# A hybrid encoder step on one core: products over 640 frames cut as 512 and 128 columns in place of 320 and 320

## The reference

```python
def swiglu(x, wg, wu, wd):
    return (jax.nn.silu(x @ wg) * (x @ wu)) @ wd

def half_ffn_block(x, wg, wu, wd, g, b):
    return layer_norm(ALPHA * x + 0.5 * swiglu(x, wg, wu, wd), g, b)
```

## Time and profile before

| | |
|---|---|
| time, median of 3 runs (lowest to highest) | 2917.87 us (2915.64 to 2918.74) |
| span of the profiled execution | 2920.5 us |
| busy share of the span: PE, PEld, DVE, ACT, POOL | 95%, 90%, 35%, 29%, 31% |
| matmul records, weight load records | 18,936 and 18,936 |
| mean granted TensorE clock | 0.968 of full speed |
| HBM traffic | 82 GB/s over the span |

### The profile page before, as it was taken

How to read it: one execution, slowest core, us unless ns; L and a number is a source line. 1 busy time by engine, 2 the same in 40 slices (tenths; PEclk the granted TensorE clock), 3 DMA queues, 4 the chain that set the end, 5 groups by cost and what they waited for, 6 DMA issues and landing times.

```text
span 2920.5 us, 49217 instructions
## 1 busy us (share of the span) xinstructions
PE 2781.7 (95%) x18936; PEld 2635.1 (90%) x18936; DVE 1026.9 (35%) x1731; ACT 846.2 (29%) x1351; POOL 914.9 (31%) x506
## 2 busy tenths in 40 slices
PE   5999999999888999999999999999999899999998
PEld 4999999898665899999999999997887688999998
DVE  2220225212555722112452212253865554211235
ACT  2221222322653332122232212223246524221222
POOL 2333333332000333333333333333133233333331
PEclk8999999999999999999999999998999999999998
DMA  9222222132347122222212222222130611222221
GB/s 154 72 83 69 72 80 73 57 111 73 131 156 265 58 65 82 76 66 78 79 51 76 81 66 79 83 62 49 44 95 1 147 51 58 74 82 67 77 83 56
DMA packets 396204, 239.64 MB, mean 82 GB/s; under 512 B 14433, under 2 KB 371025, under 8 KB 396113
## 3 DMA queue, kind: packets, MB, share of 16 engines
q1 hardware_dynamic: 396112, 238.48, 29.0%
HBM read 223.46 MB, written 14.98 MB: 82 GB/s over the span
## 4 chain that ended last, share of the span: by engine, by line
PE 88%; issue 3%; DMA 3%; ACT 2%; DVE 2%; POOL 2%; SPq 0%; DVEq 0%; ACTq 0%; POOLq 0%
PE ps L1218 73%; PE ps L1228 3%; PE ps L1311 3%; PE ps L1328 2%; PE ps L1319 1%; DMA raw<-in_ffn_w_gate 1%; PE ps L1361 1%; POOL wl L527 1%; PE ps L1286 1%; PE ps L1391 1%; PE ps L1375 1%; DVE big L888 1%; PE ps L1412 0%; ACT wh L650 0%; PE ps L1418 0%
## 5 line engine op out<-in xcount | busy, mean ns | idle before, releaser
L527 POOL TENSOR_TENSOR wl<-raw,wh 128x1024 fp32r<-128x1024 f32 (+1 forms) x296 | 779.6, 2634 | 1570.8 <-ACT wh L650 1570.8
L1218 PE MATMUL ps<-xh,wh 128*128 128x320 f32 x3488 | 797.6, 310 | 31.0 <-POOL wl L527 30.5
L1218 PE MATMUL ps<-xl,wh 128*128 128x320 f32 x3488 | 795.5, 309 | 0.0
L1218 PE MATMUL ps<-xh,wl 128*128 128x320 f32 x3488 | 795.4, 309 | 0.0
L650 ACT ACTIVATE wh<-raw 128x1024 fp32r<-128x1024 f32 (+1 forms) x298 | 335.5, 1126 | 1074.0 <-PE ps L1218 967.6
L1218 PEld LDWEIGHTS ps<-xh,wh 128*128 128x128 f32 x3488 | 583.4, 188 | 33.6 <-issue 33.0
L1218 PEld LDWEIGHTS ps<-xh,wl 128*128 128x128 f32 x3488 | 584.1, 188 | 0.0
L1218 PEld LDWEIGHTS ps<-xl,wh 128*128 128x128 f32 x3488 | 584.1, 188 | 0.0
L859 DVE SCALAR_TENSOR_TENSOR big<-big,ps 128x640 f32<-128x640 f32 x88 | 72.3, 822 | 872.7 <-PE ps L1218 850.4
L1218 PE MATMUL ps<-hl,wh 128*128 128x320 f32 x1408 | 320.8, 309 | 0.0
L1218 PE MATMUL ps<-hh,wl 128*128 128x320 f32 x1408 | 320.8, 309 | 0.0
(11 more groups left out here) (208 smaller groups left out, 2329.8 us busy)
## 6 DMA issues: line engine op xcount, KB each, us to landing
raw<-in_ffn_w_gate SPq DMA_DIRECT2D x88, 512.0 KB, 3.9
raw<-in_ffn_w_up SPq DMA_DIRECT2D x88, 512.0 KB, 3.8
raw<-in_ffn_w_down SPq DMA_DIRECT2D x64, 704.0 KB, 4.5
a_kc<-in_cache_a_k SPq DMA_DIRECT2D x16, 1024.0 KB, 5.9
a_vc<-in_cache_a_v SPq DMA_DIRECT2D x16, 1024.0 KB, 5.2
raw<-in_a_w_in SPq DMA_DIRECT2D x24, 512.0 KB, 3.7
raw<-in_b_w_in SPq DMA_DIRECT2D x16, 512.0 KB, 3.8
skewed<-big SPq DMA_DIRECT2D x1, 5248.0 KB, 54.6
```

The lines of the kernel that those rows point to most:

```text
L527: nc.gpsimd.tensor_tensor(wl[s][:, 0:kt, :], raw[s][:, 0:kt, :], wh[s][:, 0:kt, :].bitcast(F32), ALU.subtract).then_inc(w_lo[s], 1)
L1218: mm = nc.tensor.matmul(ps[:, 2 * s + c, 0:TH], w[:, k, :], x[:, k, TH * c:TH * (c + 1)], start=k == 0 and j == 0, stop=k == kt - 1 and j ...
```

## The change

The 640 frames are cut at 512 and no longer at 320. Of each product the first instruction now has 512 columns and fills bank `2*s`, the second has 128 columns and takes the start of bank `2*s+1`. The number of instructions, their weights and their order stay. The result lies in PSUM as 640 contiguous columns, so what takes it out reads one run of 640 in place of two of 320, and `two`, which folded the other operand to match, returns it as it is.

```diff
-    TH = T // 2
+    FRAMES = ((0, SEQ), (SEQ, T))
...
         def out2(s):
-            return ps[:, 2 * s:2 * s + 2, 0:TH]
+            return flat[:, 1024 * s:1024 * s + T]
...
         def two(ap):
-            return ap.rearrange("p (c n) -> p c n", c=2)
+            return ap
...
                     for j, (w, x) in enumerate(((wh[s], xa), (wh[s], xb), (wl[s], xa))):
-                        for c in range(2):
-                            mm = nc.tensor.matmul(ps[:, 2 * s + c, 0:TH], w[:, k, :], x[:, k, TH * c:TH * (c + 1)],
+                        for lo, hi in FRAMES:
+                            mm = nc.tensor.matmul(flat[:, 1024 * s + lo:1024 * s + hi], w[:, k, :], x[:, k, lo:hi],
                                                   start=k == 0 and j == 0, stop=k == kt - 1 and j == 2)
...
                     for w, x in parts:
-                        for c in range(2):
-                            mm = nc.tensor.matmul(ps[:, 2 * s + c, 0:TH], w[:, k, :], x[:, k, TH * c:TH * (c + 1)],
+                        for lo, hi in FRAMES:
+                            mm = nc.tensor.matmul(flat[:, 1024 * s + lo:1024 * s + hi], w[:, k, :], x[:, k, lo:hi],
                                                   start=k == 0 and w is wh[s] and x is xh, stop=last and x is xl)
```

## The result

The changed kernel takes 3299.2 us (3297.1 to 3304.05, 4 runs) against 2917.2 us (2915.64 to 2918.74): ratio 1.1309, 95% interval 1.1295 to 1.1323. The profiled execution's span went from 2920.5 to 3295.2 us, +374.7. The forecast was 3253 us, 46 too low and inside its range of 3170 to 3450; its sum was +335 us on the span.

The account below looks back on a forecast made before the run. PE's matmuls were taken as the bound: pairs rising from 293.2 to 337.6 ns, times 7728, gave +343 us; corrections +5, -9 and -4 made +335 on 2920.5, hence 3253 us as median, range 3170 to 3450.

Parts of the forecast that it names:

- The bound: Whole kernel: PE, busy 95% of the span, sets the end; cost changes in L1218 products reach it almost one for one.
- The 128-column half pays for a load: Short matmul of L1218: costs one weight load, 111 ns, not its stream's 67; bounds 107 and 146.6 ns.
- The 512-column half: Long matmul of L1218: 213.3 ns of streaming plus a fixed extra of 13.3 ns, 226.6 ns in all.
- The 10% bound: 512-column matmul of L1218: the extra over 2.4 GHz grows with the columns, giving 234.7 ns; used for the high end.
- Half clock: Stretches at half clock: a pair goes from 533 to 640 ns; at most some 85 pairs, +5 us.
- The cover at the start: PE's 27.4 us wait at the start for late DMA weights covers the 96 pairs or so before it, -4 us.
- Behind the norms: PE's 17.3 us wait for `xh` slices before L1228: half of 17 us added there counted as covered, -9 us.
- What would show it: Signs in the changed profile: L1218 starts alternate 0.227 and 0.111 us; a short step of 0.067 means load no bound.
- Float32's pace for a short float32r product: Rival: 128-column matmul of L1218 needs both float32 passes, 224 ns, pair 451, about 4130 us; chance 0.09.
- The load that does not bind: Rival: short matmul of L1218 costs only its stream; 2918 us, or 2755 without the extra; chance 0.07.
- The falling clock: Rival: PE less dense, so the clock drops; a tenth of pairs at half clock, +233 us, 3490; chance 0.03.
- The isolated gap: Rule for PE matmuls: columns over 2.4 GHz plus 2.5 ns, 272 ns for new and old pair, so no change.

## Why the prediction was right, and which term was off

- *The bound.* PE's products set the end: held. PE is 96% busy and its chain is L1218 and L1228 as before. 7728 pairs x (343 - 293) = 386 us, and the span grew by 374.7.
- *The 128-column half pays for a load.* Held and shown. Taking 111 ns from float32 loads of one-column matmuls, and the equal duration of 188 ns as the bridge from float32 to float32r, was right: 110 ns in the changed kernel (343 - 233), 111 ns alone. Halving the load's width removed it, and the cuts 384/256 and 448/192 fell where max(stream, load) puts them.
- *The 512-column half.* This is the term that was mis-sized: "I take 226.6", measured 233, so 6.4 ns x 7728 = 49 us. The 10% bound that I named (234.7) was the near one. The reason I gave against it was a wrong use of the earlier trace rows: a plain float32 pass takes 427 ns for 512 columns, the pace of a float32r pass at half clock, and at that pace float32r shows no extra either. So it tells nothing of an extra that shows at 213 ns. With 233 + 111 the sum is 335 + 49 = 384, 9 us over the span's growth.
- *Half clock.* The forecast of 640 ns a pair was met (0.64 us).
- *Corrections.* The cover at the start was forecast as 4 us; the wait shrank from 27.4 to 23.6 us. Behind the norms I counted 9 us as covered, but PE's idle in front of L1228 went only from 17.3 us to 14.8. With 2.5 in place of 9 the sum would be 390 or so, 16 us over the span's growth, and that rest is not resolved; the spans of the four executions, 3295.2 to 3302.1 us, differ by 7.
- *What would show it.* Here one sign was wrong. I named the starts of the matmuls as 0.227 and 0.111 us apart, and a short step of 0.067 as the sign that the load is no bound. The matmul records start 0.28 and 0.06 us apart, so by that sign the prediction would have been thrown out, although its cause was right. The steps of 0.11 and 0.23 are those of the loads. The 512-column record starts before its weights are there and seems to hold the wait for them (446 ns against 0.40 us alone), so the pair's step and the loads' timeline are what to read. The idle of the loads, named as some 40 ns a pair, is 68.3 us over 1535 pairs, 44 ns. The stretch named as 498 us for 2951 records is 510.7 for 2982, that is 505 for 2951, longer as the 512-column half is.
- *Rivals.* Float32's pace for a short float32r product (224 ns): not so, 110. The load that does not bind: not so. The falling clock: not in this change, the mean granted clock is 0.972 against 0.968. But the reason given against it, that the change adds no waits, would not have excluded it: with the 128-column matmuls alone the clock was 0.50 for 348 us in which PE's records leave no gap.
- *The rules beside it.* The Trainium skill, "TensorE: Matmul & The Clock Gate", section "LDWEIGHTS (loading the stationary operand)", gives 107 ns for 128 columns; the trace agrees at full clock (111 with what lies between two loads) and not at half clock, where it is 213 to 214. The isolated gap of the Trainium skill (same page, section "Back-to-back issue gap") would have had the two cuts equal. The section itself says that this gap has no room for the weight load and comes out too low for few columns; the runs bear that out for 128 columns of float32r (110 to 111 where the gap is 56) and have 233 for 512, where it is 216.

Left open: what the 0.03 ns a column over 2.4 GHz are (they halve neither with the load nor with the partitions). No cut of 640 columns into two can be faster than 320 and 320 by these numbers, since each is 640 x 0.45 + 2 x 2.6 = 293 ns as soon as both halves are longer than a load.

## What to carry to other kernels

When each matmul brings its own weight load, its cost is the longer of its stream and one load; here a float32r load of 128 columns is 111 ns, and pieces of 256 columns covered it while pieces of 192 and 128 did not. So keep every piece at 256 columns or more, even if the wide piece then does not fill its bank; whether the cut is even made no difference. To find this before a change, look for a load that nothing covers (a one-column matmul) and compare durations of loads, not of matmuls. To check it after, read the starts of the loads or of whole pairs: the starts of single matmul records would have said that the load was no bound. Take an extra over the nominal rate only from rows that run at the same rate.

## What the runs showed of the hardware that was not expected

- A stream of float32r columns costs 0.45 ns a column at full clock, 8% over 2.4 GHz (233 ns for 512, 146.6 for 320), and none over 1.2 GHz at half clock (0.53 us for 640 columns).
- The granted clock can stay at half while PE's matmul records leave no gap. With the 128-column matmuls alone and full loads it was 0.50 through 1302 to 1650 us, after a stretch of 16 us with the same products at 1.00 (PE busy for 13.7 of them). With half loads, PE busy for only 145.6 of 219 us, it was 0.87.
- A load of 128 weight columns repeats at 111 ns at full clock and at 214 at half clock, and one of 64 columns is short enough for 128 columns to stream at 60 and 107.
- With products over 64 of 128 partitions it was 0.50 in 200 to 300 us and 1.00 in 2000 to 2100 us, both without a gap. What decides between the two was not tried.
